# Token shift read straight from PSUM, and the two directions' 64-row products issued side by side

## The reference, cut to what matters

```
def centred_token_shift(u, mu):
    prev = jnp.pad(u[:, :-1], ((0, 0), (1, 0), (0, 0)))
    nxt = jnp.pad(u[:, 1:], ((0, 0), (0, 1), (0, 0)))
    return u + mu * (0.5 * (prev + nxt) - u)
```

```
w_raw = w0 + jnp.einsum("btdr,drc->btdc", jnp.tanh(lw), w2)
a = jax.nn.sigmoid(a0 + jnp.einsum("btdr,drc->btdc", la, a2))
```

## Time and profile before

| | |
|---|---|
| median of 3 runs | 2769.11 us (2768.67 to 2774.69) |
| the profiled execution | 2775.17 us, its span 2773.0 us |
| PE, DVE, ACT, POOL busy | 85%, 49%, 42%, 31% of the span |
| mean granted clock of TensorE | 0.918 of full speed |
| the stage's products on PE | 98 to 461 us from the span's start |
| one group (`project` beside `post`) | 43.3 to 43.8 us |

### The profile page before, as it was taken

How to read it: one execution, slowest core, us unless ns; L and a number is a source line. 1 busy time by engine, 2 the same in 40 slices (tenths; PEclk the granted TensorE clock), 3 DMA queues, 4 the chain that set the end, 5 groups by cost and what they waited for, 6 DMA issues and landing times.

```text
span 2773.0 us, 59103 instructions
## 1 busy us (share of the span) xinstructions
PE 2362.7 (85%) x25736; PEld 1683.0 (61%) x25736; DVE 1350.5 (49%) x2266; ACT 1160.6 (42%) x1933; POOL 851.1 (31%) x562
## 2 busy tenths in 40 slices
PE   8799996589889788869788888848899988889889
PEld 2677774377667676647556655526565656555556
DVE  1368788144445454441655554533444442545452
ACT  2566665233334344322544433423444443434342
POOL 0344543100010111133443433334434334443442
PEclk9899997799989999989999998969999989899999
DMA  7134544632322222222110110011111112111111
GB/s 256 61 95 130 171 126 124 185 106 79 110 73 64 73 52 70 80 85 86 65 38 31 38 39 31 23 73 65 54 46 46 46 39 88 41 46 46 46 61 61
DMA packets 148481, 211.32 MB, mean 76 GB/s; under 512 B 81920, under 2 KB 106752, under 8 KB 147456
## 3 DMA queue, kind: packets, MB, share of 16 engines
q1 hardware_dynamic: 137120, 164.28, 19.0%
q0 software_dynamic: 9952, 40.11, 4.8%
q10 hardware_dynamic: 1152, 3.15, 0.3%
HBM read 165.30 MB, written 42.21 MB: 75 GB/s over the span
## 4 chain that ended last, share of the span: by engine, by line
PE 56%; DVE 17%; POOL 10%; issue 7%; ACT 7%; DMA 2%; SPq 0%; ACTq 0%; POOLq 0%; DVEq 0%
PE ps L258 7%; PE ps L259 6%; PE ps L260 6%; PE ps L1330 2%; POOL wbl L243 2%; PE ps L540 2%; PE ps L2710 2%; PE ps L1320 2%; PE ps L2234 2%; PE ps L1345 2%; DVE Rc L335 2%; PE ps L2732 2%; DVE p L2308 1%; POOL sqc L331 1%; POOL sqc L329 1%
## 5 line engine op out<-in xcount | busy, mean ns | idle before, releaser
L243 POOL TENSOR_TENSOR wbl<-wb,wbh 128x1024 fp32r<-128x1024 f32 x128 | 306.6, 2395 | 520.6 <-ACT wbh L238 515.8
L329 POOL TENSOR_TENSOR ro<-ro 128x256 f32<-128x256 f32 (+1 forms) x16 | 16.8, 1052 | 591.5 <-DVE ro L323 591.5
L258 PE MATMUL ps<-hT2h,wbh 128*128 128x512 f32 x416 | 185.3, 445 | 6.3 <-POOL wbl L243 4.7
L258 PE MATMUL ps<-hT1h,wbh 128*128 128x512 f32 (+1 forms) x432 | 181.7, 421 | 8.5 <-POOL hT1l L2379 4.4
L258 PE MATMUL ps<-hTh,wah 128*128 128x512 f32 (+1 forms) x512 | 178.7, 349 | 9.9 <-issue 6.4
L259 PE MATMUL ps<-hTl,wah 128*128 128x512 f32 (+1 forms) x512 | 173.3, 339 | 0.0
L260 PE MATMUL ps<-hTh,wal 128*128 128x512 f32 (+1 forms) x512 | 172.7, 337 | 0.0
L259 PE MATMUL ps<-hT2l,wbh 128*128 128x512 f32 x416 | 166.3, 400 | 0.0
L260 PE MATMUL ps<-hT2h,wbl 128*128 128x512 f32 x416 | 166.1, 399 | 0.0
L238 ACT ACTIVATE wbh<-wb 128x1024 fp32r<-128x1024 f32 x128 | 134.2, 1049 | 68.8 <-PE ps L1929 43.5
L243 POOL TENSOR_TENSOR wal<-wa,wah 128x1024 fp32r<-128x1024 f32 x34 | 108.3, 3186 | 166.8 <-ACT wah L238 166.8
(11 more groups left out here) (404 smaller groups left out, 5996.2 us busy)
## 6 DMA issues: line engine op xcount, KB each, us to landing
wb<-in_w_in SPq DMA_DIRECT2D x56, 512.0 KB, 3.4
s_str_dram<-s POOLq DMA_DIRECT2D x48, 576.0 KB, 8.7
wm<-in_ada SPq DMA_DIRECT2D x48, 512.0 KB, 4.6
bkv<-s_str_dram SPq DMA_DIRECT2D x96, 192.0 KB, 3.5
wa<-in_rw_in SPq DMA_DIRECT2D x34, 512.0 KB, 4.0
wb<-in_da_in SPq DMA_DIRECT2D x32, 512.0 KB, 3.4
ARI<-s_str_dram SPq DMA_DIRECT2D x96, 128.0 KB, 3.5
wb<-in_w_out SPq DMA_DIRECT2D x16, 512.0 KB, 3.5
```

The lines of the kernel that those rows point to most:

```text
L243: e.tensor_tensor(self.lo[:, n % 2], self.raw[:, n % 3], self.hi[:, n % 2].bitcast(F32), ALU.subtract).then_inc(self.K.s.w_lo, 1)
L258: e.matmul(z, wh[:, k, :], hi[:, k, a:b], start=k == 0, stop=False)
```

## The change

A bank of a mixed product is no longer copied to a padded row. ACT writes `dst = (1 - mu) * psum` at once, scaling while it reads PSUM. DVE then adds `mu/2` times the bank shifted by one column to the right, and then to the left, in place. These are two instructions a bank and four a product, each reading PSUM and `dst`, the second waiting for the first. Both work by bank and no longer by product: the context half is done at P1, P4, P7 and the latent half at P3, P6, P9. The bank is free for PE when DVE's second addition is done (`mix_done`, now counted twice a product). The pads, the sum row and POOL's six memsets of the pads' end columns are gone.

The decay and `la` products are cut at column 512 (`HALVES`, 512 and 256 columns) where they were cut at 256, and the loops are exchanged: the outer one is over the columns, the inner over the directions. Direction 0 has its operands on partitions 0 to 63 and direction 1 on 64 to 127, and each direction now has a bank of its own. The first half of both directions is issued at p1 (decays) and p5 (`la`), the second at p2 and p6. The sigmoids follow the same order; DVE's scan of direction 0 waits for the third sigmoid of its group where it waited for the second.

```diff
     def pe_product(self, e, n):
         def free(j):
-            if 2 * n + j >= 4:
-                e.wait_ge(K.s.evac_a, 2 * n + j - 3)
+            if n >= 2:
+                gp, z = divmod(n - 4, 4)
+                if n >= 4 and z == 3:
+                    e.wait_ge(K.s.evac_a, 2 * gp + j + 1)
+                else:
+                    e.wait_ge(K.s.mix_done, 2 * (n - 2 if n < 4 else 2 + 3 * gp + z) + j + 1)
...
     def act_mix(...):
...
             e.wait_ge(s.prod, self.W.prod(n, j))
-            if m >= 2:
-                e.wait_ge(s.mix_done, m - 1)
-            elif j == 0:
-                e.wait_ge(s.pad_zero, 6)
-            o = 1 if a == 0 else 2
-            e.activation(pad[:, a + o:b + o], K.psum[:, (2 * n + j) % 4, 0:b - a], ACT.Copy).then_inc(s.evac_a, 1)
+            e.activation(dst[:, a:b], K.psum[:, (2 * n + j) % 4, 0:b - a], ACT.Copy,
+                         scale=self.omu[:, 0, mucol:mucol + 1]).then_inc(s.mix_own, 1)
         yield from product_steps(self.cols, sink)
-        e.wait_ge(s.evac_a, 2 * n + 2)
-        for (a, b), o in zip(self.cols, (0, 1)):
-            e.activation(dst[:, a:b], pad[:, a + o + 1:b + o + 1], ACT.Copy,
-                         scale=self.omu[:, 0, mucol:mucol + 1]).then_inc(s.mix_own, 1)
 
     def dve_mix(self, e, n, m, mucol, dst):
-        yield from product_steps(self.cols, lambda j, a, b: None)
-        e.wait_ge(s.evac_a, 2 * n + 2)
-        e.tensor_tensor(ss[:, 0:769], pad[:, 0:769], pad[:, 2:771], ALU.add).then_inc(s.mix_sum, 1)
-        for j, ((a, b), o) in enumerate(zip(self.cols, (0, 1))):
-            t = e.scalar_tensor_tensor(out=dst[:, a:b], in0=ss[:, a + o:b + o],
-                                       scalar=self.omu[:, 1, mucol:mucol + 1], in1=dst[:, a:b], op0=ALU.mult,
-                                       op1=ALU.add)
-        t.then_inc(s.mix_done, 1)
+        K, s, mu = self.K, self.K.s, self.omu[:, 1, mucol:mucol + 1]
+        def sink(j, a, b):
+            z, v = K.psum[:, (2 * n + j) % 4, 0:b - a], 2 * m + j + 1
+            e.wait_ge(s.mix_own, v)
+            e.scalar_tensor_tensor(out=dst[:, a + 1:b], in0=z[:, 0:b - a - 1], scalar=mu, in1=dst[:, a + 1:b],
+                                   op0=ALU.mult, op1=ALU.add).then_inc(s.mix_sum, 1)
+            e.wait_ge(s.mix_sum, v)
+            e.scalar_tensor_tensor(out=dst[:, a:b - 1], in0=z[:, 1:b - a], scalar=mu, in1=dst[:, a:b - 1],
+                                   op0=ALU.mult, op1=ALU.add).then_inc(s.mix_done, 1)
+        yield from product_steps(self.cols, sink)
...
-    def pe_decays(self, e, gp, d):
-        s, n = self.K.s, 4 * gp + 2 * d
-        for j, (a, b) in enumerate(self.cols):
-            if n:
-                e.wait_ge(s.sg_sig, n + j - 1)
-            e.matmul(self.K.psum[:, 6 + j, 0:b - a], self.lw2[64 * d:64 * d + 64, 0, 128 * gp:128 * gp + 128],
+    HALVES = (0, 512), (512, 768)
+
+    def pe_decays(self, e, gp, x):
+        s, n, (a, b) = self.K.s, 4 * gp + 2 * x, self.HALVES[x]
+        if n:
+            e.wait_ge(s.sg_sig, n)
+        for d in range(2):
+            e.matmul(self.K.psum[:, 6 + d, 0:b - a], self.lw2[64 * d:64 * d + 64, 0, 128 * gp:128 * gp + 128],
                      self.tl[64 * d:64 * d + 64, a:b], start=True, stop=True).then_inc(s.sg_mm, 1)
...
     pe_post, the `la` products (p5, p6):
-        for d in range(2):
-            for j, (a, b) in enumerate(self.cols):
-                if d == 0:
-                    e.wait_ge(self.rs.m, self.rs.done(2 * gp + j))
-                else:
-                    e.wait_ge(s.a_sig, 4 * gp + j + 1)
-                e.matmul(K.psum[:, 4 + j, 0:b - a], ...
+        for x, (a, b) in enumerate(self.HALVES):
+            if x == 0:
+                e.wait_ge(self.rs.m, self.rs.done(2 * gp + 1))
+            else:
+                e.wait_ge(s.a_sig, 4 * gp + 2)
+            for d in range(2):
+                e.matmul(K.psum[:, 4 + d, 0:b - a], ...
...
     dve_post:
-            e.wait_ge(s.sg_sig, 4 * gp + 2 * d + 2)
+            e.wait_ge(s.sg_sig, 4 * gp + d + 3)
             e.tensor_tensor_scan((self.er if d == 0 else self.wp)[:, d], self.keep[:, :], self.wp[:, d], 0.0, ALU.mult,
```

More of the change, by code:

```diff
@@ L622, in __init__ @@
         self.st_out, self.bg_out = (K.s.st_out0, K.s.st_out1), (K.s.bg_out0, K.s.bg_out1)
-        K.count("evac_a", 68)
+        K.count("evac_a", 16)
     def pe_product(self, e, n):
@@ L638, in pe_first, with act_mix @@
                                                  enumerate(self.cols)], lambda k: self.norm.wait_lo(e, k))
-    def act_mix(self, e, n, m, mucol, dst, gp=None, bonus=0):
-        K, s, i = self.K, self.K.s, m % 2
-        pad = self.pads[i]
+    def act_mix(self, e, n, m, mucol, dst, gp=None, bonus=0, made=0):
+        K, s = self.K, self.K.s
         if n:
@@ L659, in act_mix @@
-        if bonus:
-            e.wait_ge(s.bonus_out, bonus)
-        e.wait_ge(s.evac_a, 2 * n + 2)
-        for (a, b), o in zip(self.cols, (0, 1)):
-            e.activation(dst[:, a:b], pad[:, a + o + 1:b + o + 1], ACT.Copy,
-                         scale=self.omu[:, 0, mucol:mucol + 1]).then_inc(s.mix_own, 1)
-    def dve_mix(self, e, n, m, mucol, dst):
-        K, s, i = self.K, self.K.s, m % 2
-        pad, ss = self.pads[i], self.ss
-        yield from product_steps(self.cols, lambda j, a, b: None)
-        e.wait_ge(s.evac_a, 2 * n + 2)
-        if m:
-            e.wait_ge(s.mix_done, m)
-        e.tensor_tensor(ss[:, 0:769], pad[:, 0:769], pad[:, 2:771], ALU.add).then_inc(s.mix_sum, 1)
-        e.wait_ge(s.mix_sum, m + 1)
-        for j, ((a, b), o) in enumerate(zip(self.cols, (0, 1))):
-            e.wait_ge(s.mix_own, 2 * m + j + 1)
-            t = e.scalar_tensor_tensor(out=dst[:, a:b], in0=ss[:, a + o:b + o],
-                                       scalar=self.omu[:, 1, mucol:mucol + 1], in1=dst[:, a:b], op0=ALU.mult,
-                                       op1=ALU.add)
-        t.then_inc(s.mix_done, 1)
+            if j == 0:
+                if m == 0:
+                    e.wait_ge(s.omu_made, 2)
+                if gp is not None:
+                    self.stored(e, gp)
+                if made:
+                    e.wait_ge(s.kd_made, made)
+                if bonus:
+                    e.wait_ge(s.bonus_out, bonus)
@@ L700, in act_project @@
         for z, (n, m, mucol, dst) in enumerate(self.mixes(gp)):
-            yield from self.act_mix(e, n, m, mucol, dst, gp if z else None, 2 * gp - 2 if z == 2 and gp >= 2 else 0)
+            yield from self.act_mix(e, n, m, mucol, dst, gp if z else None, 2 * gp - 2 if z == 2 and gp >= 2 else 0,
+                                    4 * gp - 4 if z == 0 and gp >= 2 else 0)
         n = 5 + 4 * gp
@@ L753, in act_decays @@
             e.wait_ge(s.prd_v, 8 * gp - 2)
-        for d in range(2):
-            for j, (a, b) in enumerate(self.cols):
-                e.wait_ge(s.sg_mm, 4 * gp + 2 * d + j + 1)
+        for x, (a, b) in enumerate(self.HALVES):
+            for d in range(2):
+                e.wait_ge(s.sg_mm, 4 * gp + 2 * x + d + 1)
                 K.table[0] = "sig"
-                e.activation(self.chunks(self.wp[:, d], 1, a, b), self.by_chunk(K.psum[:, 6 + j, 0:b - a]), ACT.Sigmoid,
+                e.activation(self.chunks(self.wp[:, d], 1, a, b), self.by_chunk(K.psum[:, 6 + d, 0:b - a]), ACT.Sigmoid,
                              bias=K.Q("w0", 8 * d + gp, 1)).then_inc(s.sg_sig, 1)
@@ L778, in pe_post @@
         yield
-        for d in range(2):
-            for j, (a, b) in enumerate(self.cols):
-                if d == 0:
-                    e.wait_ge(self.rs.m, self.rs.done(2 * gp + j))
-                else:
-                    e.wait_ge(s.a_sig, 4 * gp + j + 1)
-                e.matmul(K.psum[:, 4 + j, 0:b - a], self.lw2[64 * d:64 * d + 64, 1, 128 * gp:128 * gp + 128],
+        for x, (a, b) in enumerate(self.HALVES):
+            if x == 0:
+                e.wait_ge(self.rs.m, self.rs.done(2 * gp + 1))
+            else:
+                e.wait_ge(s.a_sig, 4 * gp + 2)
+            for d in range(2):
+                e.matmul(K.psum[:, 4 + d, 0:b - a], self.lw2[64 * d:64 * d + 64, 1, 128 * gp:128 * gp + 128],
                          self.la[64 * d:64 * d + 64, a:b], start=True, stop=True).then_inc(s.la_mm, 1)
@@ L802, in act_post @@
         k, kk = self.kb[gp % 2], K.Q("kk", gp, 1)
-        e.wait_ge(s.mix_done, 3 + 3 * gp)
+        e.wait_ge(s.mix_done, 2 * (3 + 3 * gp))
         if gp:
@@ L823, in act_post @@
         yield
[L824 to L827, removed]
+        for x, (a, b) in enumerate(self.HALVES):
+            for d in range(2):
+                e.wait_ge(s.la_mm, 4 * gp + 2 * x + d + 1)
                 K.table[0] = "sig"
-                e.activation(bd[:, a:b], K.psum[:, 4 + j, 0:b - a], ACT.Sigmoid,
+                e.activation(S9[:, 3 * d, a:b], K.psum[:, 4 + d, 0:b - a], ACT.Sigmoid,
                              bias=K.Q("a0", 8 * d + gp, 1)).then_inc(s.a_sig, 1)
```

(18 more changed lines are left out.)

6 lines of the change are left out of this document (removed).

## The result

The changed kernel took 2809.76 us (median of 4 runs, 2807.4 to 2811.64) against 2771.9 (2768.67 to 2776.28): 1.35% slower, ratio 1.0135, 95% interval 1.0116 to 1.0154. The prediction was 2767 us with a range of 2755 to 2780. Its profiled execution took 2811.64 us, span 2809.8.

What follows compares the result with a forecast made beforehand. It took a circle over DVE and POOL, almost level with PE, as the bound: 43.56 us a turn against 43.54. Changes outside and five turns at +0.02 summed to -2.0 us from 2773.2, median 2767 us, range 2755 to 2780.

Steps and rivals of the forecast that it cites:

- What the order does: Step on P4 standing ahead of p3 in DVE's queue: circle becomes one group, 43.56 us against 43.54.
- the 43.56 of the prediction: Turn from P4 to P4 over DVE and POOL: 4.62 + 30.19 + 8.75 us.
- DVE from first scan to last product: DVE's part of the circle: 32.33 us less one POOL stop of 2.14, so 30.19 us.
- ACT's piece and DVE's pair: At P4 before the first scan: scaled copy 0.47, 0.04 to DVE, pair of additions 0.93 us.
- The 64-row products: Decays and la on PE: row halves overlap, 1.05 and 0.63 us, saving 2.58 us a group.
- The scan into `wp`: DVE scan no longer held by POOL's `wal`: 1.8 us instead of 3.9, 2.14 us less.
- The additions from PSUM: DVE's twelve new additions a group are free of POOL; 0.485 us for 256 columns, 0.746 for 512.
- PE's saving: 2.58 us a group on PE, expected to stay hidden by the circle over DVE and POOL.
- PE would stand idle there for some 2 us: Before P4: PE comes some 2 us early and waits for POOL's `wal`.
- 1.0 us was expected from tanh: Stage start: tanh no longer behind ACT's scaled copies of 1.12 us, so PE's third product 1.0 us earlier.
- The slower one: POOL's `wal` of v still falls on a DVE scan: turn 45.7 us, total 2780 us; chance 23%.
- The rival with PE's saving coming through in a circle of two groups: Two-group circle stays: 42.25 us a turn, total 2760, or 2750 with one POOL stop less; 27% for both.

Runs made afterwards that it cites:

- halves-only kernel: Kernel before the change with only the new 64-row decay and la products, padded mix kept; 2774.65 us, ratio 0.9994 to before.
- mix only: Changed kernel with the decay and la products, and DVE's scan wait, as before the change; 2803.92 us, ratio 1.0104 to before.
- own r kernel: Changed kernel with r in its own pair of rows, so its context half at P4 waits for no store; ratio 1.0017 to before.
- late r: Changed kernel with both halves of the r mix taken out of PSUM at P6 on ACT and DVE; ratio 0.9966 to before.

## Why the prediction was wrong

**The step that failed** is "What the order does". It listed what the context half of r needs at P4: 24 matmuls, ACT's piece, DVE's pair. The kernel has another condition in the same branch, `if gp is not None: self.stored(e, gp)`, now ahead of the activation. The prediction gives this wait no term and no reason for leaving it out. The buffer was last used two groups before, which sounds like more than a turn ago. But `project(gp+1)` runs beside `post(gp)` and waits for the stores of group gp-1, and these leave at p8, right before P1. Counted from the written order, they are one pass back, 8.4 us before P4, and land 18.1 us after the first is issued. In the kernel before this fitted: the wait came at P7, and the stores were down. The circle is then 18.06 + 1.43 + 30.27 + 0.30 us, and the 43.56 of the prediction is hidden inside it. As a term of the prediction's own sum, with 3.18 us from P4 to ACT's copy, the wait is 18.06 - 8.44 - 3.18 = 6.44 us: 43.56 + 6.44 = 50.0 us a turn, 50.16 measured.

**What held.** DVE from first scan to last product: 30.19 predicted, 30.27 measured. ACT's piece and DVE's pair, from ACT's start: 0.47 + 0.04 + 0.93 = 1.44 predicted, 1.43 measured. The 64-row products: 1.05 and 0.63 us from start to start predicted; 1.06 and 0.64 measured (342.62 - 341.56, and 346.67 - 346.03 in the halves-only kernel), 1.13 and 0.70 long. The scan into `wp` is free of POOL, 1.76 us. The additions from PSUM at 399.06 and 399.84 took 0.75 us each inside POOL's two `wal` of 5.82 us. The rule of the Trainium skill (SBUF — State Buffer, "Who interferes with whom") is that a DVE instruction with at most one SBUF input does not contend with GpSimd, and one with two does when GpSimd reads SBUF. The trace agrees: L335 and L891, with two, took 2.74 and 3.16 us beside POOL. That PE's saving buys nothing while the circle does not pass over PE is borne out by mix only against changed, where it bought nothing. No run takes the halves out of the own r kernel, whose circle is the predicted one.

**What was off besides.** Once the store wait is taken away, the turn is 44.30 us, not 43.56. PE's half clock after its idle time before P4 makes 0.6 of the 0.7 us (1.5 us in two turns of five). The prediction saw that PE would stand idle there for some 2 us and priced what follows at nothing. At the stage's start 1.0 us was expected from tanh; it began at 103.92 against 104.11, as DVE's second addition now ends last (ACT waited 0.45 us for it), while the first products had ended 0.56 us later in this execution.

**The rivals.** The slower one had the sign but not the place: it put a POOL stop on the scan, 2.1 us a turn, and that stop did go away. The real wait was in none of the cases. The rival with PE's saving coming through in a circle of two groups is near what late r does (42.2 to 42.8 us for 42.25), but not what the changed kernel does.

## What to carry to other kernels

When an intermediate copy is taken out, list every wait of the instruction that now does both jobs, and place each in the queue: the copy had let the engine go on before its destination was free. For each buffer wait, find in the written order when the last reader is issued, and add its time to landing; "two buffers ago" can be less than one pass. If it must stay, move it behind the work that does not need it, which here made the difference between 1.0135 and 0.9966.

## What the runs showed of the hardware

- Six stores of 576 KB issued by POOL in 5.98 us took 18.06 us from the first issue to the last landing, 3.5 MB.
- Two fp32 matmuls on different 64-row halves overlap: 1.13 us for 2 x 512 columns and 0.70 for 2 x 256, where 256 and 512 columns of one half took 1.55.
- In the own r kernel the granted clock fell to half for 3.4 us (0.60 in the window shown) in one turn and not in the next, though PE had stood idle for 2.1 us in either; the runs do not say what decides it. The kernel before, with PE idle for at most 1.1 us there (200 to 440 us), showed no such fall.
- A low part of POOL's that met a DVE instruction with two SBUF inputs cost DVE some 2 us (3.16 us for 0.95 at L891).
